# Routing the tokens of tiles 0 and 1 while tile 3's output products run, and moving half of the first expert's row selection

## The reference

```python
def route(hf, w_router, b_router):
    logits = (hf @ w_router).astype(jnp.float32) + b_router.astype(jnp.float32)
    probs = jax.nn.softmax(logits, axis=-1)
    grouped = probs.reshape(t, N_GROUPS, EXPERTS_PER_GROUP)          # 4 groups of 4 experts
    group_score = lax.top_k(grouped, TOP_K)[0].sum(-1)
    sel_group = jnp.argmax(group_score, axis=-1)
    in_group = jnp.take_along_axis(grouped, sel_group[:, None, None], axis=1)[:, 0]
    top_p, top_local = lax.top_k(in_group, TOP_K)                    # 2 experts a token
    ...

for l in range(DEPTH):
    ...
    x = x + g1[:, None, :] * mixer(h, w_in[l], w_ret_o[l], pool_w[l], pool_scale[l], w_pool_o[l], w_out[l])
    h = modulate(rmsnorm(x, norm2_g[l]), sh2, sc2)
    x = x + g2[:, None, :] * moe(h, w_router, b_router, w_gate[l], w_up[l], w_down[l])
return rmsnorm(x, final_g)
```

## Time and profile before

| what | value |
|---|---|
| runs | 1478.89, 1476.23, 1477.74 us |
| median | 1477.74 us |
| span of the profiled execution, first to last instruction | 1475.1 us |
| profiled execution's own time | not given apart from its span; the median of the runs is 2.6 us above that span |
| TensorE matmul busy | 1440.2 us, 98% |
| VectorE busy | 1132.6 us, 77% |
| ScalarE busy | 767.0 us, 52% |
| GpSimd busy | 151.6 us, 10% |
| TensorE's mean granted clock | 0.995 of full |
| bytes moved | 377.49 MB, 256 GB/s in the mean |

### The profile page before, as it was taken

The page is one execution under the profiler, slowest core; times in us unless marked ns, Lnnn a source line. Parts: engine busy times, 40 slices in busy tenths (PEclk is TensorE's granted clock), DMA queues, the critical chain, the costliest instruction groups (busy, mean ns, idle before and its releaser), DMA issues.

```text
span 1475.1 us, 18818 instructions
## 1 busy us (share of the span) xinstructions
PE 1440.2 (98%) x6815; PEld 1152.1 (78%) x6815; DVE 1132.6 (77%) x1538; ACT 767.0 (52%) x1102; POOL 151.6 (10%) x139
## 2 busy tenths in 40 slices
PE   7999999999999999999989999999999999999996
PEld 2788877778878878888758888878888778888884
DVE  5774786555669999999977657854345899999998
ACT  4343433222347878777623344242233587778773
POOL 0000001000012211111100000100000122112010
PEclk9999999999999999999999999999999999999998
DMA  9855556455557999999956543642243879999995
GB/s 355 307 184 188 176 196 209 144 175 172 186 218 290 392 362 398 379 382 378 354 205 204 193 133 115 206 138 87 85 172 145 322 293 387 377 380 395 371 373 210
DMA packets 107413, 377.49 MB, mean 256 GB/s; under 512 B 16521, under 2 KB 16713, under 8 KB 106548
## 3 DMA queue, kind: packets, MB, share of 16 engines
q1 hardware_dynamic: 90864, 331.39, 61.3%
q0 software_dynamic: 15200, 40.62, 7.6%
q10 hardware_dynamic: 1252, 4.22, 0.9%
HBM read 361.32 MB, written 34.64 MB: 268 GB/s over the span
## 4 chain that ended last, share of the span: by engine, by line
PE 80%; DVE 13%; DMA 2%; ACT 2%; issue 2%; DVEq 1%; SPq 0%; ACTq 0%; POOLq 0%; POOL 0%
PE ps L1786 24%; PE ps L1788 23%; PE ps L1787 23%; DVE w_lo L1528 4%; DVE w_lo_more L1528 2%; PE ps L1871 2%; PE ps L2049 1%; DMA gate_row<-mod_rows 1%; PE ps L2098 1%; PE ps L1940 1%; DVE xgT_lo L1514 1%; ACT w_hi L837 1%; DVE y_out L1551 1%; PE ps L1944 1%; DMA raw<-w 1%
## 5 line engine op out<-in xcount | busy, mean ns | idle before, releaser
L1008 DVE TENSOR_TENSOR w_lo<-raw,w_hi 128x1024 fp32r<-128x1024 f32 x132 | 161.4, 1224 | 212.7 <-ACT w_hi L652 211.5
L652 ACT ACTIVATE w_hi<-raw 128x1024 fp32r<-128x1024 f32 x132 | 139.1, 1058 | 333.2 <-PE ps L1788 332.5
L1528 DVE TENSOR_TENSOR w_lo<-raw,w_hi 128x1024 fp32r<-128x1024 f32 x184 | 217.1, 1218 | 2.2 <-DMA gate_row<-mod_rows 1.3
L1786 PE MATMUL ps<-w_hi,hT_lo 128*128 128x512 f32 x512 | 206.9, 404 | 3.2 <-DVE hT_lo L1111 2.5
L1528 DVE TENSOR_TENSOR w_lo_more<-raw,w_hi_more 128x1024 fp32r<-128x1024 f32 x176 | 207.9, 1218 | 1.3 <-ACT w_hi_more L837 0.4
L1788 PE MATMUL ps<-w_hi,hT_hi 128*128 128x512 f32 x512 | 200.0, 391 | 0.0
L1787 PE MATMUL ps<-w_lo,hT_hi 128*128 128x512 f32 x512 | 199.6, 390 | 0.0
L837 ACT ACTIVATE w_hi<-raw 128x1024 fp32r<-128x1024 f32 x184 | 187.4, 1057 | 10.0 <-DMA raw<-w 5.4
L837 ACT ACTIVATE w_hi_more<-raw 128x1024 fp32r<-128x1024 f32 x176 | 178.9, 1056 | 8.4 <-DMA raw<-w 6.3
L1786 PE MATMUL ps<-hT_hi,w_lo 128*128 128x512 f32 x320 | 130.5, 408 | 0.0
L1788 PE MATMUL ps<-hT_hi,w_hi 128*128 128x512 f32 x320 | 125.0, 390 | 0.0
(11 more groups left out here) (286 smaller groups left out, 2632.1 us busy)
## 6 DMA issues: line engine op xcount, KB each, us to landing
raw<-w SPq DMA_DIRECT2D x590, 512.0 KB, 6.1
h_rows<-h POOLq DMA_DIRECT2D x8, 1024.0 KB, 4.9
ahead<-w SPq DMA_DIRECT2D x4, 2048.0 KB, 11.9
x_state<-x POOLq DMA_DIRECT2D x2, 2048.0 KB, 10.3
y_rows<-x_in ACTq DMA_DIRECT2D x4, 1024.0 KB, 11.9
x<-x_state POOLq DMA_DIRECT2D x4, 1024.0 KB, 7.1
pair_early<-y_rows SPq DMA_DIRECT2D x4, 1024.0 KB, 6.8
x<-x_in SPq DMA_DIRECT2D x4, 512.0 KB, 14.1
```

What stands on the lines that cost most here:

```text
L652: act.activation(w_hi[:, q % W_SLOTS], stream_piece(l, q, r), ACT.Copy).then_inc(w_hi_ready, 1)
L1008: v.tensor_tensor(w_lo[:, q % W_SLOTS], stream_piece(l, q, r), w_hi[:, q % W_SLOTS], ALU.subtract).then_inc(raw_used, 1)
L1528: v.tensor_tensor(ring_lo(e * EXP + n), expert_piece(e, n), ring_hi(e * EXP + n), ALU.subtract).then_inc(raw_used, 1)
L1786: pe.matmul(dst, a_lo, b_hi, start=start, stop=False)
```

## The change

On TensorE, the partial sums of tiles 0 and 1 run inside tile 2's products (ahead of its last piece), their logits ahead of tile 3's products. Behind the last product come the partial sums of tile 2, the positions of the tokens of tiles 0 and 1, the logits of tiles 2 and 3, and the half of the row selection that belongs to tiles 0 and 1, with 5 fillers instead of 16. After the second choice come the positions of tiles 2 and 3, the counts, and the other half of the row selection.

On VectorE, the choice is now made twice, each time for two tiles. The first stands around the read of tile 2. The modulated rows of tile 2 are made behind the read of tile 3, after the one-hot matrices of tiles 0 and 1. The first scaling of tile 3's rows stands behind the second choice.

On ScalarE the exponentials are taken in two halves, the first among the deviations of the tiles, with the tables loaded for exponential and again for square root.

```diff
+SOON = 2
@@ scalar @@
+            def exponentials(l, t0, t1):
+                act.wait_ge(max_off, l * 2 + (2 if t0 else 1))
+                act.activation(probs[:, NE * t0:NE * t1], lg[:, NE * t0:NE * t1], ACT.Exp).then_inc(exp_done, 1)
...
                 for t in range(NT):
+                    if t == SOON:
+                        act.activation(spare[:], k("eps"), ACT.Exp)
+                        exponentials(l, 0, SOON)
+                        act.drain()
+                        act.activation(spare[:], k("eps"), ACT.Sqrt)
...
@@ vector @@
+            def route_soon(l):
+                parts_copy(l, 0, SOON)
+                v.wait_ge(logits_ready, l * 3 + 1)
+                for t in range(SOON):
+                    token_logits(t)
+                largest_off(0, SOON)
...
             def route_tokens(l):
-                v.wait_ge(logits_ready, l * 2 + 1)
-                for t in range(NT - 1):
-                    token_logits(t)
+                parts_copy(l, SOON, NT - 1)
+                first_hots(l, 0, SOON)
+                norm_tile(l, 1, "h2", NT - 2)
+                v.wait_ge(logits_ready, l * 3 + 2)
+                token_logits(NT - 2)
                 inverse_deviation(l * 8 + 4, NT - 1)
-                last_h2_scaled(0)
-                v.wait_ge(logits_ready, l * 2 + 2)
+                v.wait_ge(logits_ready, l * 3 + 3)
                 token_logits(NT - 1)
...
+                largest_off(SOON, NT)
+                choose(l, SOON, NT)
                 v.tensor_scalar(best[:], ranks[:], 0.0, None, ALU.is_equal)
                 v.tensor_scalar(second[:], ranks[:], 1.0, None, ALU.is_equal)
...
+                last_h2_scaled(0)
+                first_hots(l, SOON, NT)
                 last_h2_shifted(0).then_inc(h2_half, 1)
                 last_h2_scaled(1)
...
-                for t in range(NT):
+                for t in range(SOON):
                     read_output(l, 1, t)
-                    if t < NT - 1:
-                        norm_tile(l, 1, "h2", t)
...
+                    norm_tile(l, 1, "h2", t)
+                route_soon(l)
+                read_output(l, 1, NT - 2)
+                choose(l, 0, SOON)
+                read_output(l, 1, NT - 1)
                 route_tokens(l)
@@ tensor @@
+                    if g == NGROUP - 1 and t == SOON and j == 3:
+                        pe.wait_ge(ada_row_ready, l * NADA + columns(l))
+                        router_parts(l, 0, SOON)
+                    if g == NGROUP - 1 and t == NT - 1 and j == 0:
+                        pe.wait_ge(early_parts_copied, l * 2 + 1)
+                        for early in range(SOON):
+                            one = router_logits(l, early)
+                        one.then_inc(logits_ready, 1)
...
-                router_parts(l, 0, 3)
+                router_parts(l, SOON, NT - 1)
+                pe.wait_ge(acc_free, acc_value(l, NGROUP - 1, 1))
+                pe.wait_ge(chosen_ready, l * 2 + 1)
+                pe.matmul(ps[:, 0, 0:NE * SOON], before_r[:], chosen[:, 0:NE * SOON], start=True, stop=False)
+                pe.matmul(ps[:, 0, NE:NE * SOON], ones_r[:], chosen[:, 0:NE], start=False, stop=True).then_inc(pos_ready, 1)
                 x_transposes(l, NT - 1, [1])
...
                 router_logits(l, 3).then_inc(logits_ready, 1)
-                keep_busy(16)
+                units_done(l, "h2")
+                first_rows_selected(l, range(SOON))
+                keep_busy(5)
...
-                first_rows_selected(l)
+                first_rows_selected(l, range(SOON, NT))
```

More of the change, by code:

```diff
@@ new lines, in choose @@
+            def choose(l, t0, t1):
+                cols = slice(NE * t0, NE * t1)
+                groups = slice(NG * t0, NG * t1)
+                beaten_by(beats[:, 4 * NE * t0:4 * NE * t1].rearrange("p (s n) -> p s n", n=16),
+                          lg[:, cols].rearrange("p (s e) -> p s e", e=4))
+                v.tensor_reduce(ranks[:, cols], beats[:, 4 * NE * t0:4 * NE * t1].rearrange("p (a b) -> p a b", b=4), AX, ALU.add)
+                v.drain()
+                v.wait_ge(exp_done, l * 2 + (2 if t0 else 1))
+                v.scalar_tensor_tensor(rt[:, cols], ranks[:, cols], 1.0, probs[:, cols], ALU.is_le, ALU.mult)
+                v.drain()
+                v.tensor_reduce(s4[:, groups], rt[:, cols].rearrange("p (s e) -> p s e", e=4), AX, ALU.add)
+                v.tensor_scalar(two[:, cols], ranks[:, cols], 1.0, None, ALU.is_le)
+                v.drain()
+                beaten_by(group_beats[:, cols].rearrange("p (t n) -> p t n", n=16),
+                          s4[:, groups].rearrange("p (t g) -> p t g", g=NG))
+                v.tensor_reduce(group_rank[:, groups], group_beats[:, cols].rearrange("p (a b) -> p a b", b=4), AX, ALU.add)
+                v.drain()
+                in_best_group(chosen[:, cols], two, t0, t1).then_inc(chosen_ready, 1)
+                in_best_group(chosen_f[:, cols], two, t0, t1)
@@ new lines, in first_hots @@
+            def first_hots(l, t0, t1):
+                v.wait_ge(pos_ready, l * 3 + (2 if t0 else 1))
+                src = ps[:, 7, 0:NE * (t1 - t0)] if t0 else ps[:, 0, 0:NE * t1]
+                v.tensor_copy(pos[:, NE * t0:NE * t1], src)
+                v.drain()
+                for t in range(t0, t1):
+                    v.tensor_scalar(hot0[:, t], k("iota"), pos[:, NE * t:NE * t + 1], chosen_f[:, NE * t:NE * t + 1],
+                                    ALU.is_equal, ALU.mult).then_inc(hot0_ready, 1)
@@ L1370, in route_tokens @@
[L1370 to L1378, removed]
@@ L1394, in route_tokens @@
-                in_best_group(hots[:, 64:128], second)
+                in_best_group(hots[:, 0:64], best, 0, NT)
+                in_best_group(hots[:, 64:128], second, 0, NT)
                 v.drain()
@@ L1982, in misc, with first_rows_selected @@
                     retention(l)
-            def first_rows_selected(l):
+            def first_rows_selected(l, tiles):
                 for j in range(2):
-                    for t in range(NT):
+                    for t in tiles:
                         if j == 0:
@@ L2200, in _ @@
                     group_tile(l, NGROUP - 1, t)
-                pe.wait_ge(ada_row_ready, l * NADA + columns(l))
-                router_parts(l, 0, 3)
-                x_transposes(l, NT - 1, [1])
-                pe.wait_ge(acc_free, acc_value(l, NGROUP - 1, 1))
-                pe.wait_ge(early_parts_copied, l + 1)
-                for t in range(3):
-                    one = router_logits(l, t)
-                one.then_inc(logits_ready, 1)
-                router_parts(l, 3, 4)
+                router_parts(l, SOON, NT - 1)
[3 more added lines that the diff above has]
+                pe.matmul(ps[:, 0, NE:NE * SOON], ones_r[:], chosen[:, 0:NE], start=False, stop=True).then_inc(pos_ready, 1)
+                x_transposes(l, NT - 1, [1])
+                pe.wait_ge(early_parts_copied, l * 2 + 2)
+                router_logits(l, 2).then_inc(logits_ready, 1)
+                router_parts(l, NT - 1, NT)
                 pe.wait_ge(parts_copied, l + 1)
@@ L2212, in _ @@
                 router_logits(l, 3).then_inc(logits_ready, 1)
-                keep_busy(16)
-                pe.wait_ge(chosen_ready, l + 1)
-                pe.matmul(ps[:, 7, 0:NE * NT], before_r[:], chosen[:], start=True, stop=False)
-                for s in range(1, NT):
-                    one = pe.matmul(ps[:, 7, NE * s:NE * NT], ones_r[:], chosen[:, 0:NE * (NT - s)], start=False, stop=s == NT - 1)
-                one.then_inc(pos_ready, 1)
+                units_done(l, "h2")
+                first_rows_selected(l, range(SOON))
+                keep_busy(5)
+                pe.wait_ge(chosen_ready, l * 2 + 2)
+                pe.matmul(ps[:, 7, 0:NE * SOON], before_r[:], chosen[:, NE * SOON:NE * NT], start=True, stop=False)
+                pe.matmul(ps[:, 7, 0:NE * SOON], ones_r[:], chosen[:, NE:NE * 3], start=False, stop=False)
+                pe.matmul(ps[:, 7, 0:NE * SOON], ones_r[:], chosen[:, 0:NE * 2], start=False, stop=False)
+                pe.matmul(ps[:, 7, NE:NE * SOON], ones_r[:], chosen[:, 0:NE], start=False, stop=True).then_inc(pos_ready, 1)
                 for s in range(NT):
```

58 lines of the change are left out of this document (23 added, 35 removed).

## The result

The changed kernel takes 1485.4 us (median of 4 runs, 1482.17 to 1488.54), the kernel before 1477.38 (4 runs): ratio 1.0053, interval 1.0039 to 1.0067. That is +8.0 us, slower as forecast, but nearly twice the forecast +4.1 and above the range's end of 1484.8.

The account below looks back on a forecast made before the run. TensorE is busy nearly throughout, but the chain through last modulated row, gate row and gather was taken to decide. Layer delays of 2.2 + 1.9 = +4.1 us on the 1477.74 median gave 1481.8 us, range 1479.0 to 1484.8.

Parts of the forecast that it names:

- What bounds the kernel: Last output products to first expert: the chain through last modulated row, gate row and gather decides, not TensorE's row selection.
- Inserted work, S = 1.8: Router work between TensorE's products makes the last product 1.8 us later in each layer, bounds 1.2 and 2.2.
- the two pieces: Partials of tiles 0 and 1 inside tile 2's products, 1.1 us; two logits before tile 3's products, 0.7 us.
- VectorE, D = 2.2 to 2.3: On VectorE behind the routing, the last modulated rows are ready 2.2 to 2.3 us later, at 442.4 instead of 440.13.
- ScalarE's table loads: Two more loads of 1.28 us each before tile 2's transposes are copied; cost nothing, cover 0.5 us.
- Downstream: GpSimd's queue: tile 2's store done before 442; gate row and gather merely shift, passing on 2.2 and 1.9 us by layer.
- Rival 1: Before the expert loop: the gate row lands sooner after its issue, absorbing part; +2.3 us, 1480.0; chance 0.20.
- Rival 2: Before expert 0: TensorE's shorter row selection decides, start 0.9 us earlier a layer, say 1475.3; chance 0.10.
- Rival 3: TensorE idles about 2 us before expert 0 and its clock falls; +0.9 us a layer, 1483.6; chance 0.12.
- The sum: Delays of 2.2 us in the first layer and 1.9 us in the second make +4.1 us, 1481.8 us.
- case 3: TensorE's clock falls before expert 0; with the inserted work at its upper bound it set the range's end of 1484.8.

Follow-up runs that it names:

- a_gate_early: The changed kernel with the gate row fetched as soon as the last tile is added, ahead of the stores of tiles 2 and 3; 1482.08 us, ratio 1.0033.
- b_store_late_gate: The kernel before with tile 2's store held until the maximum is off and the gate row fetched ahead of it, once the last tile is added; 1475.93 us.
- b_store_late: The kernel before with only GpSimd's store of tile 2 held back until the maximum is off; 1484.29 us, ratio 1.0049.
- b_store_late_act: The kernel before with tile 2's store issued late by ScalarE on its own queue, behind the routing's exponential; 1484.77 us, ratio 1.0046.
- after: The changed kernel itself, with the whole change and no further edit; 1485.4 us, ratio 1.0053 to the kernel before.
- b_rows_late: The kernel before with only tile 2's modulated rows moved behind the parts copy that follows the last tile's read; 1483.57 us, ratio 1.0046.
- a_rows_early: The changed kernel with tile 2's modulated rows made ahead of the last tile's read again; 1485.42 us, ratio 1.0049.
- b_few_fillers: The kernel before with 4 fillers instead of 16 on TensorE while VectorE chooses; 1481.19 us, ratio 1.0027.

## Why the prediction was wrong, and where it was right

**What bounds the kernel** held: the path through the last modulated row, the gate row and the gather decides, not the row selection. TensorE's shorter selection won 0.84 us up to expert 0 in layer 1, and nothing at the end.

**Inserted work, S = 1.8:** 1.73 in the trace; 1.07 and 0.51 were the two pieces. Alone, +2.7 for both layers. Right.

**VectorE, D = 2.2 to 2.3:** the last rows were done at 442.87 against 440.13, less 0.56: 2.18. The choice came at 438.63 (forecast 438.2, and 0.56 of that is the execution's own). ScalarE's table loads cost nothing. Right.

**Downstream: the step that failed.** It said of the store of tile 2 that it "moves from 426 to about 434.5, when the two early weight transfers are also in flight, but it is done before 442", and then let gate row and gather move by D. The issue time was right (435.30); the rest was not. The store took 11.8 us instead of 7.3, since its megabyte went through DMA engines that are nearly full (share 0.93 to 1.04 in each 4 us from 434 to 450), and landed at 447.1. So it was still in flight when the gate row was issued at 444.16, and in layer 1 the gate row moved by D and by 3.26 more (10.93 - 7.67), with 0.32 us of slack on VectorE. The late store alone costs the kernel before 7.1 us; getting the gate row out of its way gives the changed kernel 3.1 to 3.3 back.

**The two don't add up**, 2.7 + 7.1 being more than 8.0. In the changed kernel TensorE reaches expert 0 late anyway, and in layer 2 of the profiled execution the gate row was in time. Its four runs lie 6.4 us apart, those of the kernel before 2.7; that the gate row is late in some layers of some executions fits this, but only profiled executions show it.

**Rival 1 (partly absorbed, 0.20)** wanted the gate row to land sooner after its issue. In layer 2 of the profiled execution it did, 7.0 us instead of 8.1, and VectorE's wait of 0.98 was gone; in layer 1 it took 3.26 us longer, and that decided. By its own terms the rival's sum is 1.5 + 0.5 and not 1.5 + 0.8. **Rival 2 (a gain, 0.10)** fell with the wait of 1.53. **Rival 3 (the clock falls, 0.12)** was right in that the clock fell, and wrong in its place: 1.5 us of idleness ahead of expert 0 left it at 1.00 (behind 1.95 us at the layers' border it was 0.63), but it fell behind the gate row's wait (3.97 us, then 0.52) and, in layer 2, behind three gaps of 0.68, 0.28 and 0.40 us between small matmuls (then 0.50). It lengthens the selection by 1.43 us there. The same three gaps left the clock at 1.00 in layer 1, and in both layers of a_gate_early. The rival's +0.9 us a layer is shown by no run: it was the author's estimate. What the runs show in its place is this 1.43 us in layer 2, and in layer 1 at most some 1.8 us behind the gate row's wait (6.7 - 0.89 - 3.97).

**The sum:** +4.1 was forecast for what turned out to be +4.9 when the gate row is kept in time. The other 3.1 are the late gate row with the clock's fall behind it. Of the 4.9, 2.7 is the inserted work; the 2.2 left are VectorE's later rows and the gather (waits of 1.73 and 0.74), not measured apart, since every run that moved the rows alone also moved the clock. That 4.1 and 4.9 lie so near is in part luck: the forecast had 3.6 for the inserted work and 0.5 for the rest. The early gate row also takes away waits that the kernel before still has, worth up to the 1.7 us of b_store_late_gate, so the change by itself may cost more than 4.9. The upper end of the range does not follow from its own words either, case 3 with S at its bound being 1484.4 and not 1484.8; the measured time is above both.

**Open:** what brings the clock down. 1.60 us without work did it in the runs with the rows early (0.50 behind it), and 1.5 us ahead of expert 0 never did (1.00). But the length of the stretch does not decide by itself, as layer 1 of b_store_late shows, where 2.17 us left the clock at 1.00:

```profile
453.18 0.50 PE L1786 MATMUL ps<-w_hi,xgT_lo 128*128 128x512 f32 x1 [2.17 <-DVE w_lo L1528]
```

```profile
454.00:458.00 4.00, 4.00 (x20) 3.28 (x19) 3.48 (x7) 1.55 (x3) 2.34 (x2) 1.00 1.00 384
```

The places differ in what ran before, but no run varied that alone.

## What to carry to other kernels

When a step moves, move its transfers in the sum too, and take their time from the stretch in which they now run: a store that was free in a gap can still be in flight when the next fetch is issued, and delay it (by up to 3.4 us here, for a megabyte), from GpSimd's queue as from ScalarE's. Where the fetch on which the next work waits can be issued earlier, ahead of such bytes, do that; here it turned a loss of 7.1 us into a gain of 1.7. And fillers are counted against the wait that they must cover, not against the work that they replace: 4 instead of 16 left 3.13 us of idleness here, and cost 4.5.

## What the runs showed of the hardware

- In b_store_late a store moved from a stretch with DMA share 0.59 into one at 1.02 took 11.1 us instead of 7.3 and made a 512 KB fetch, issued 8.4 us behind it, take 10.26 us instead of 7.67 on the same queue, and 9.75 when the store was on ScalarE's queue (b_store_late_act). Issued 9.7 us or more behind such a store, in three kernels whose clock had fallen (after, b_rows_late, a_rows_early), the fetch took 7.0 to 8.1 us.
- Idle stretches of 1.60 us (a_rows_early), 2.01 (b_rows_late) and 3.13 (b_few_fillers) on TensorE were followed by a granted clock near 0.50 for some 3 to 7 us; the row selection then took 6.00 instead of 3.82 us (32 records), and 8.60 and 9.22 instead of 7.32 (64 records). After 1.53 us of idleness ahead of expert 0 it stayed at 1.00, and after 2.17 us ahead of the remainder in layer 1 of b_store_late as well.
- Removing 12 matmuls whose result nobody reads made the kernel 4.5 us slower (b_few_fillers).
